# Half of the second block's gate products, made in pieces inside three earlier stages of a two-block kernel

## What is computed

```python
h = rms_norm(x, g_mix)
proj = h @ w_in                       # queries, keys, values of three branches
y_sb  = stick_breaking_attention(...) @ w_o_sb    # 8 heads of 64
y_dil = dilated_mixture(...) @ w_o_dil            # 12 heads of 64 in 3 groups
y_mem = memory_attention(...) @ w_o_mem           # 4 heads of 128, 256 memory rows
gates = sigmoid(h @ w_gate + b_gate).reshape(B, S, 3, 1024)
merged = gates[:,:,0] * y_sb + gates[:,:,1] * y_dil + gates[:,:,2] * y_mem
x = x + merged @ w_out
```

## Time and profile before

| | |
|---|---|
| time, median of 3 runs | 2958.86 us (2958.85 to 2959.19) |
| profiled execution, span | 2956.1 us; its time is taken as the median, 2.8 us more |
| PE, DVE, ACT, POOL busy | 2831.6, 2034.7, 1374.0, 412.1 us |
| mean granted TensorE clock | 0.976 of full |

### The profile page before, as it was taken

How to read it: one execution, slowest core, us unless ns; L and a number is a source line. 1 busy time by engine, 2 the same in 40 slices (tenths; PEclk the granted TensorE clock), 3 DMA queues, 4 the chain that set the end, 5 groups by cost and what they waited for, 6 DMA issues and landing times. The chain is left out here.

```text
span 2956.1 us, 36707 instructions
## 1 busy us (share of the span) xinstructions
PE 2831.6 (96%) x13991; PEld 2389.1 (81%) x13991; DVE 2034.7 (69%) x3249; ACT 1374.0 (46%) x2168; POOL 412.1 (14%) x293
## 2 busy tenths in 40 slices
PE   7999999899999999978999999999999989999999
PEld 5757888578888679866778789999999988878887
DVE  4575532498888517765433488999897868888886
ACT  4336521377777517664322333356667633323232
POOL 0000000010100000000000000111122324554542
PEclk9999999799999999969999999999999999999999
DMA  4100272567776511100123223667778979999996
GB/s 164 51 23 1 86 176 76 235 242 294 276 292 252 225 57 60 71 29 22 61 91 125 106 104 116 217 228 276 271 274 313 354 283 388 381 391 390 395 383 262
DMA packets 162398, 594.19 MB, mean 201 GB/s; under 512 B 15408, under 2 KB 86704, under 8 KB 133936
## 3 DMA queue, kind: packets, MB, share of 16 engines
q1 hardware_dynamic: 103472, 429.79, 39.8%
q0 software_dynamic: 41472, 138.45, 12.6%
q10 hardware_dynamic: 17280, 23.60, 2.2%
HBM read 560.81 MB, written 68.71 MB: 213 GB/s over the span
## 5 line engine op out<-in xcount | busy, mean ns | idle before, releaser
L2351 POOL DMA_INDIRECT RG<-in_un,EI x128 | 178.2, 1392 | 1297.1 <-DVE EI L2603 899.7
L2351 POOL DMA_INDIRECT RG<-in_vn,EI x128 | 187.7, 1467 | 267.0 <-DVE X L2365 240.8
L2722 PE MATMUL bank<-VH,GL 128*128 128x512 f32 x768 | 208.5, 393 | 0.4 <-DVE GL L2417 0.4
L2718 PE MATMUL bank<-VH,GH 128*128 128x512 f32 x768 | 208.0, 392 | 0.0
L2365 DVE SCALAR_TENSOR_TENSOR X<-RG,DG,X 128x1024 f32<-128x1024 f32 x128 | 164.2, 1283 | 54.4 <-DMA RG<-in_vn,EI 50.8
L2362 DVE CUSTOM_DVE_ANT_0 RG<-RG,HR 128x1024 f32<-128x1024 f32 x128 | 156.6, 1223 | 32.0 <-DMA RG<-in_un,EI 30.0
L2332 PE MATMUL bank<-HTl,UH1r 128*128 128x384 f32 x512 | 177.1, 346 | 0.0
L2332 PE MATMUL bank<-HTl,UH0r 128*128 128x384 f32 x512 | 175.8, 343 | 0.3 <-ACT UH0r L2317 0.3
L2333 PE MATMUL bank<-HTh,UH1r 128*128 128x384 f32 x512 | 173.0, 338 | 0.0
L2333 PE MATMUL bank<-HTh,UH0r 128*128 128x384 f32 x512 | 171.4, 335 | 0.0
L2722 PEld LDWEIGHTS bank<-VH,GL 128*128 128x128 f32 x768 | 144.1, 188 | 33.3 <-DVE GL L2417 0.9
(11 more groups left out here) (675 smaller groups left out, 7664.4 us busy)
## 6 DMA issues: line engine op xcount, KB each, us to landing
UR<-in_u SPq DMA_DIRECT2D x64, 1024.0 KB
VR<-in_vn SPq DMA_DIRECT2D x32, 2048.0 KB, 10.2
UP<-in_wup SPq DMA_DIRECT2D x22, 2048.0 KB, 8.2
DN<-in_wdn SPq DMA_DIRECT2D x32, 1024.0 KB, 7.3
W<-in_weights SPq DMA_DIRECT2D x12, 2048.0 KB, 8.4
W<-in_weights SPq DMA_DIRECT2D x16, 1536.0 KB, 7.2
wspill<-VR SPq DMA_DIRECT2D x12, 2048.0 KB, 7.6
aspill<-GA ACTq DMA_DIRECT2D x120, 192.0 KB
```

Source lines behind the costliest of these rows:

```text
L2351: e.indirect_dma_start(RG[q % RR], None, d["un" if what == "u" else "vn"][:, :], off).then_inc(*row_in[q % RR].up(16))
L2718: e.matmul(bk, r(gh[:, a, t]), r(vh[:, a, :]), start=g == 0 and a == 0, stop=False)
L2722: e.matmul(bk, r(gl[:, a, t]), r(vh[:, a, :]), start=False, stop=False)
```

## The change

Of the 8 gate units, units 0 to 3 (`g`, each of 3 branches, 12 sets `s`) get their gate products ahead of the gate stage, in 96 pieces `p` of three matmuls: 24 pieces in steps 28 to 39 of the stick stage (two a step), 55 in the 55 steps of the dilated stage (`FILL`: two a step in steps 0 to 9, one in 10 to 13, 16 to 23, 26 to 33 and 40 to 54), 11 and 6 in the mix. The eight warm-up matmuls of the mix and the ten at the head of the gate stage go. Each set is split by ScalarE and VectorE (1024 columns; steps 27, 29, 31, 35, 39 of the stick stage, steps 0, 4, 8, 14, 24, 34, 48 of the dilated stage), its bank copied to SBUF (VectorE in the stick stage in steps 32, 36, 40, ScalarE behind it in steps 4, 8, 14, 24, 34, 48 and the mix) and stored to DRAM (`gs`, 256 KB a set). `att_m` gets one output bank instead of two and pauses two steps after every fourth unit. In the gate stage four blocks of gate products are each followed by the branch products of two units, one with its gates made there, one with gates read back. The first of these weights is split at the mix's end. Cut to the core:

```diff
 class Attention:
+            def at(self, slot):
+                i, h = divmod(slot, self.heads + self.pause)
+                return self.heads * i + h if slot >= 0 and h < self.heads else -1
...
-                n = step - 6
+                n = self.at(step - 6)
...
+            EB = (4, 5, 4, 7, 6, 7, 7, 7, 6, 7, 6, 7)
+            def load_early(e, g):
+                e.dma_start(ER[g % 2][0].rearrange("p k n -> p (k n)"), w_src(31 + 2 * g)).then_inc(*er_in[g % 2].up(16))
+            def act_early(e, s):
+                g, b = divmod(s, 3)
+                e.wait_ge(*er_in[g % 2](16 * (g // 2) + 16))
+                e.wait_ge(*(e_mm(s - 2) if s >= 3 else j_mm(24)))
+                e.activation(r(EH[:, :, span(b)]), ER[g % 2][0][:, :, span(b)], ACT.Copy).then_inc(*e_hi.up(1))
+            def dve_early(e, s):
+                g, b = divmod(s, 3)
+                e.wait_ge(*e_hi(s + 1))
+                e.tensor_tensor(r(ER[g % 2][1][:, :, span(b)]), ER[g % 2][0][:, :, span(b)], EH[:, :, span(b)], ALU.subtract).then_inc(*e_lo.up(1))
+            def pe_early(e, p):
+                s, k = divmod(p, 8)
...
+                if k == 0:
+                    e.wait_ge(*e_lo(s + 1))
+                    if early_prior(s) >= 0:
+                        e.wait_ge(*e_out(early_prior(s) + 1))
+                e.matmul(bk, r(lo), r(HTh[:, k, :]), start=k == 0, stop=False)
+                e.matmul(bk, r(hi), r(HTl[:, k, :]), start=False, stop=False)
+                i = e.matmul(bk, r(hi), r(HTh[:, k, :]), start=False, stop=k == 7)
...
+            def store_early(e, s):
+                e.wait_ge(*e_out(s + 1))
+                e.dma_start(d["gs"][s], ZG[s % 2]).then_inc(*z_done[s % 2].up(16))
 stick stage, TensorE
                             pe_jobs(e, step)
+                            if 28 <= step < 40:
+                                for p in range(2 * step - 56, 2 * step - 54):
+                                    pe_early(e, p)
 dilated stage, SP
+                        e.wait_ge(*e_mm(3))
+                        load_early(e, 2)
                         for tb in range(4):
                             e.dma_start(MS[tb], d["mqs"][span(tb), :]).then_inc(*mq_in[tb].up(16))
...
+                        for s in range(3, 12):
+                            store_early(e, s)
+                            if s == 5:
+                                load_early(e, 3)
+                            if s == 8:
+                                e.wait_ge(*e_mm(9))
+                                load_gate(e, 0)
+                                e.wait_ge(*att_d.scored(48))
+                                load_branch(e, 0)
+                        for n in range(2):
+                            e.wait_ge(*z_done[n](96))
 dilated stage, TensorE and ScalarE
                             pe_memory(e, step)
+                            for p in range(filled[step], filled[step + 1]):
+                                pe_early(e, p)
                             att_d.pe(e, step)
...
+                            if step in SPLITS:
+                                act_early(e, SPLITS[step])
+                            if step in OUTS:
+                                act_early_out(e, OUTS[step])
                             act_memory(e, step)
 mix
-                    warm(e, 8, 7)
+                    for p in range(filled[-1], 90):
+                        pe_early(e, p)
                     e.wait_ge(*x_w(1))
...
+                    for p in range(90, 96):
+                        pe_early(e, p)
...
                     e.activation(att_d.RI, att_d.RS, ACT.Ln).then_inc(*x_ln.up(1))
+                    act_early_out(e, REST[0])
+                    act_gate_split(e, 0, LW0)
                     e.wait_ge(*x_off(1))
 gate stage
+            UNIT = (4, 0, 5, 1, 6, 2, 7, 3)
+                def load_early_gates(self, e, n):
+                    if n >= 3:
+                        e.wait_ge(*self.y_lo(n - 1))
+                        e.wait_ge(*self.y_sum(n - 1))
+                    for b in range(3):
+                        e.dma_start(self.SG[1][b], d["gs"][3 * UNIT[n] + b]).then_inc(*self.z_in[b].up(16))
+                def sync(self, e):
+                    load_gate(e, 1)
+                    load_branch(e, 1)
+                    self.load_early_gates(e, 1)
+                    load_gate(e, 2)
+                    for n in range(2, 8):
+                        if n == 4:
+                            load_gate(e, 3)
+                        if n == 6:
+                            e.wait_ge(*l_gated(9))
+                            e.dma_start(self.OUT[0][0], w_src(47)).then_inc(*self.out_in[0].up(16))
+                        load_branch(e, n)
+                        if n % 2:
+                            self.load_early_gates(e, n)
+                    e.wait_ge(*l_gated(12))
+                    e.dma_start(X, d["xs"].rearrange("(b p) n -> p b n", p=128)).then_inc(*in_x.up(16))
+                    e.wait_ge(*l_projected(24))
+                    e.dma_start(self.OUT[1][0], w_src(48)).then_inc(*self.out_in[1].up(16))
+                def pe(self, e):
+                    for i in range(4):
+                        self.pe_gates(e, i)
+                        self.pe_project(e, 2 * i)
+                        self.pe_project(e, 2 * i + 1)
...
+                def act_sigmoid(self, e, n):
+                    for b in range(3):
+                        g = self.SG[n % 2][b]
+                        if n % 2:
+                            e.wait_ge(*self.z_in[b](16 * (n // 2) + 16))
...
+                        e.activation(g, g if n % 2 else bank[(3 * (n // 2) + b) % 4], ACT.Sigmoid,
+                                     bias=gg("bg2")[:, 8 * b + UNIT[n]:8 * b + UNIT[n] + 1]).then_inc(*self.sig.up(1))
-                g2 = Gates(c1, "2", lambda m: 31 + 2 * m, (47, 48), [((oTs, oTsl), 4, lambda m: (32 + 2 * m, 0)), ((oTd, oTdl), 2, lambda m: (32 + 2 * m, 512)),
+                g2 = Late(c1)
```

More of the change, by code:

```diff
@@ L409, in pe @@
                     self.wait_kept(e, n)
-                    if h == 0 and i >= 2:
-                        e.wait_ge(*self.stored(i - 1))
-                    o = self.banks[2 + i % 2][:, span(h, self.width)]
+                    if h == 0 and i >= self.kept:
+                        e.wait_ge(*self.stored(i - self.kept + 1))
+                    o = self.outs[i % self.kept][:, span(h, self.width)]
                     for j in range(nb):
@@ L474, in act @@
                         e.wait_ge(*self.flipped(i + 1))
-                        self.store(e, i, self.banks[2 + i % 2])
-                n = step - 4
+                        self.store(e, i, self.outs[i % self.kept])
+                n = self.at(step - 4)
                 if 0 <= n < self.n and n % 2 == 0:
@@ new lines, in program @@
+            er_in, z_done = [sem(f"er_in{n}", True) for n in range(2)], [sem(f"z_done{n}", True) for n in range(2)]
+            e_hi, e_lo, e_mm, e_out = (sem(n, True) for n in ("e_hi", "e_lo", "e_mm", "e_out"))
+            EB = (4, 5, 4, 7, 6, 7, 7, 7, 6, 7, 6, 7)
+            early_prior = lambda s: max([x for x in range(s) if EB[x] == EB[s]], default=-1)
+            def load_early(e, g):
+                e.dma_start(ER[g % 2][0].rearrange("p k n -> p (k n)"), w_src(31 + 2 * g)).then_inc(*er_in[g % 2].up(16))
@@ L2058, in _ @@
                         e.dma_start(BD, d["bd"]).then_inc(*bd_in.up(16))
-                        load_weights(e, 33)
+                        e.wait_ge(*j_mm(24))
+                        load_early(e, 0)
+                        e.wait_ge(*j_mm(28))
+                        load_early(e, 1)
+                        for s in range(3):
+                            store_early(e, s)
                     @block.tensor
@@ L2078, in _ @@
                             dve_jobs(e, step)
+                            if step in EARLY_AT:
+                                dve_early(e, EARLY_AT.index(step))
+                            if step in (32, 36, 40):
+                                s = (step - 32) // 4
+                                wait_early_out(e, s)
+                                e.tensor_copy(ZG[s % 2], bank[EB[s]]).then_inc(*e_out.up(1))
             release()
@@ L2131, in program @@
                                   lambda i, h, j: mv[:, j, span(h)], lambda i: 256, None, float(128 ** -0.5), 128,
-                                  [mt2[:, span(n, 256)] for n in range(3)], [mt2[:, span(n, 256)] for n in (3, 4)], [mt2[:, 1536:2048]], oTm)
+                                  [mt2[:, span(n, 256)] for n in range(3)], [mt2[:, span(n, 256)] for n in (3, 4)], [mt2[:, 1536:2048]], oTm, bank[6:7], 2)
                 NORM0, ATT0 = 2, 10
+                STEPS = att_d.steps()
+                FILL = [2] * 10 + [1] * 4 + ([0] * 2 + [1] * 8) * 2 + [0] * 6 + [1] * (STEPS - 40)
+                filled = [24 + int(x) for x in np.cumsum([0] + FILL)]
```

(22 more changed lines are left out.)

243 lines of the change are left out of this document (219 added, 24 removed).

## The result

The changed kernel takes 2908.2 us (median of 4 runs, 2905.8 to 2913.1); its time is 0.9842 of the kernel before's, with an interval of 0.9826 to 0.9858: some 47 us saved by that ratio, where 42 was forecast. Its profiled execution has a span of 2907.2 us against 2956.1.

A forecast was written before the change was run, and what follows sets the result against it. It took TensorE, busy 2831.6 of 2956.1 us, as the bound. Terms +5 + 6 + 10.5 + 4.5 + 2 - 70.0 = -42.0 us took 2958.9 to 2916.9, predicted as 2917 us, range 2898 to 2942.

The forecast's parts named there:

- likeliest case: Whole kernel: the summed forecast of -42.0 us, to 2917 us; chance 0.55.
- Nearly free: Stages receiving pieces: full clock makes insertions cost about +14 instead of +28; -56, 2903 us; chance 0.22.
- Pay twice: VectorE and ScalarE: each of 12 splits costs 2.0 us, pieces of steps 10 to 54 on the path; 2943 us; chance 0.17.
- Slower: Stick tail and dilated stage: TensorE stays at half clock, kernel 17 us slower, 2976 us; chance 0.04.
- Gate stage: 288 gate products leave at 0.231 us each, gaps shrink to about 2 us plus 1: 168.0 us, gain 70.0.
- Stick tail: 24 pieces and splits delay ScalarE and VectorE, full clock gives up to 3.4 us back: +5 us.
- Steps 0 to 9: Dilated stage: weight load delays the query rows by +4, subtractions of steps 4 and 8 add more: +6 us.
- Steps 10 to 39: Dilated stage: TensorE limits; 20 pieces add 13.9 us, less slack, plus splits: +10.5 us.
- The 2.5 for the splits: Steps 10 to 39: three subtractions (steps 14, 24, 34) and the copies precede short chains: +2.5 us.
- this slack covers about 6 us: Steps 10 to 39: dilated-only steps of 1.01 us leave TensorE half idle, covering about 6 us of the pieces.
- Steps 40 to 54: Dilated stage's end: one piece a step, partly covered by the chain's latency: +4.5 us.
- Mix: Eleven pieces free in place of the warm-up, selection at half clock, six pieces behind it delay the gates: +2 us.

The follow-up runs named there:

- experiment 6: Changed kernel with the rounding copy and subtraction of early sets 6 to 11 cut to 8 columns a row block; 2907.0 us.
- experiments 1: Changed kernel with the four query loads issued ahead of the 1536 KB weight load at the dilated stage's head; 2903.9 us.
- experiment 3: Changed kernel with memory attention pausing one step instead of two after every fourth unit; 2906.9 us.
- Experiment 2: Changed kernel with the last six pieces ahead of TensorE's wait before the selection instead of behind the selection; 2901.1 us, ratio 0.9817 to the kernel before.
- 7: Changed kernel with query loads ahead of the weight load and the last six pieces ahead of the selection; 2896.2 us, ratio 0.9813 to the kernel before.
- 8: As 7, with VectorE's subtraction of the first gate weight ahead of its wait for the first selection bank; 2895.9 us, ratio 0.9807 to the kernel before.
- 12: The same kernel as 8, run again; 2899.7 us, ratio 0.9823 to the kernel before.
- experiment 4: Changed kernel with one product in each piece instead of three, splits, copies, stores and waits kept; 2898.2 us.
- experiment 11: As 8, with seven unused products of rounded float32 behind the selection matmuls; 2894.8 us, ratio 0.9812 to the kernel before.

## Why the prediction was right, point by point

The likeliest case held, with its size 5 us short, and none of the rivals. "Nearly free" asked for a cost of 14 and it was 28.2 (3.1 + 5.4 + 14.5 + 3.8 + 1.4), 28 forecast. That the two sums are so close is luck: steps 10 to 39 cost 4.0 more than forecast and the four other stretches 3.8 less together. "Pay twice" wanted 2.0 a split; 0.8 was measured over the six splits that experiment 6 took out. "Slower" wanted half clock in the tail, which was at 1.00.

- *Gate stage, -70 forecast, -72.8 measured.* The 288 products left at 0.231 as counted. The gaps, which I left at 2 plus 1 for the missing warm-up, fell to about 0.2, because the clock had risen at 1435.42, during the pieces ahead of the stage. That is luck: in experiments 1 and 6, with the same pieces there, it had not risen yet and the stage took 168.9; in experiment 3 it had, and the stage took 166.2; without them (2, 7, 8, 12) it took 167.6 to 169.0. The forecast of 168.0 ends with the last product; on the scale of these figures, which end 1.0 later, it is 169.0. So the size is right for a stage begun at half clock, but for another reason: there the 3 us above the products are the slow clock and not gaps.
- *Stick tail, +5 forecast, +3.1 measured.* The mechanism was right: TensorE at half clock was the limit up to the last row copy, and full clock paid for the pieces. It was so for the last 8.6 us and not 6.7, so the clock gave back more, some 4.3 us of TensorE's time (an estimate) instead of 3.4, against the 4.2 of the 18 products there: TensorE's stretch came out 0.15 us longer, for +0.8. The splits were mis-sized: at the last exponential they made 1.8 instead of 2.9, and only 0.8 of that delayed the start of TensorE's stretch (25.17 us after the last projection job, 24.35 before), the rest lay beside its work. Together 1.0 instead of 3.7. The end was +2.0 instead of +1.3.
- *Steps 0 to 9, +6 forecast, +5.4 measured.* The load ahead of the query rows was forecast at +4 and cost 4.8, of which the other order gave 3.3 to 3.7 back. From the first squares on the steps took 30.7 us instead of 30.0: the splits of steps 4 and 8, forecast at 2.2, cost 1.2, and pieces and clock together gave about 0.6 back, where nothing was forecast.
- *Steps 10 to 39, +10.5 forecast, +14.5 measured: the term that was mis-sized.* The 2.5 for the splits was right (2.6 measured). What failed is "this slack covers about 6 us". It covered about 2.8 (13.9 less the 11.1 estimated from experiment 4), and spreading the memory units, which I costed at nothing, cost at least the 0.6 of experiment 3, which took out half of it. 11.1 + 2.6 + 0.6 is 14.3 of the 14.5; the close agreement rests on that estimate and on a half-measured term. Windows of the kernel before would have told, of the whole stretch and of its last steps, where dilated attention runs alone:

```profile
...
1316.53:1368.38 51.85, 49.32 (x335) 45.00 (x336) 31.50 (x138) 32.97 (x133) 0.00 (x0) 1.00 0.01 1
```

```profile
...
1359.50:1368.38 8.88, 7.17 (x48) 5.76 (x48) 4.82 (x29) 5.75 (x26) 0.00 (x0) 1.00 0.01 3
```

  TensorE was idle for only 2.5 us of the stretch, and busy for four fifths of its last steps, not half; the step of 1.01 us that I used is measured in the earlier trace rows behind step 40, in another stage. In the changed kernel TensorE is idle for 4.5 us there (66.37 less 61.88), with the small splits of experiment 6 for 2.0. So its busy time grew by 12.6 us, the splits added 2.5 us of idle time, and the pieces filled hardly any of it.
- *Steps 40 to 54, +4.5 forecast, +3.8 measured*, 0.9 of it the split of step 48.
- *Mix, +2 forecast, +1.4 measured.* The chain to the selection did not move (15.0 and 15.4 us), the eleven pieces were free, and the selection stayed at half clock, as assumed. Experiment 2 shows that the six pieces behind it were more than the whole cost: ahead of it, the stretch is 28.3 us, 5.9 shorter than before.

By the Trainium skill (DMA: Bandwidth & Descriptors, Queues, rings and completion order) one ring takes its descriptors in order; the trace agrees, as the query rows landed 7.1 us after their issue behind the 1536 KB load and after 2.5 us ahead of it. By the Trainium skill (TensorE: Matmul & The Clock Gate, What's actually happening) activity releases the clock; the clock column agrees, with 0.70, 0.86 and 1.00 over the stick tail as none, two and six fillers a step were added.

## What to carry over

Products moved into a stage are free only where TensorE waits for others: here they cost nothing in the stick tail up to TensorE's last wait, and about four fifths of their time in a stretch where TensorE was already 95% busy, so read the slack from the stretch's busy time, not from single steps. A time that does not move when both load and clock are changed proves nothing about either: in the last 8.6 us of the tail 19 added products and a doubled clock cancelled, which a window of TensorE over that stretch shows at once. Look at both sides of a moved block: which small load now queues behind its big one, and whether its last pieces could stand in front of a wait instead of behind it; these two edits returned 7.8 us, a sixth of what the change had saved. A clock that falls in one stage is paid in the next, so judge an edit of 1 to 3 us by its stages, not by the whole time.

## What the runs showed of the hardware

- Matmuls added to a gapless stretch at half clock can be paid by the clock: in the stick tail 40 matmuls took 8.62 us at 0.50, the same with 19 more of 128x512 8.78 us at 1.00. Ahead of that stretch ScalarE's and VectorE's chain took 24.35 us at a mean clock of 0.81, 0.91 and 1.00.
- The selection matmuls (4 contraction rows) took 10.6 us for twelve when made at half clock throughout, after 5.65 us without work, 7.8 to 9.1 when begun at full clock after 1.5 us without work; the clock then fell while they ran, although TensorE had work without a gap (the window of experiment 11 over them, 1415.33 to 1423.16, has it busy throughout at a mean of 0.68).
- Seven products of unrounded float32, each recorded as two matmuls, took 9.3 us at a mean clock of 0.67; seven rounded ones at the same place took 3.35 us at 0.50.
- A 256 KB load issued 0.38 us behind one of 1536 KB took 7.1 us to land, issued ahead of it 2.5; the big one took 8.4 us instead of 6.9 when the small ones went first.
